# Weight places of a streamed mixture of experts: one w1 place for even and one for odd experts, one w2 place

## The reference

```
x = x + merged @ w_out
hf = rmsnorm(x, norm_ffn_g)
top_vals, top_idx = top_k(hf @ w_router + b_router, 4)     # of 32 experts
gates = softmax(top_vals)
# for each expert e, on the tokens that chose it (64 slots here):
gu  = xb @ w1[e] + b1[e]                # w1[e] is 1024 x 2048, 8 MB
act = (clip(up) + 1) * min(gate, 7) * sigmoid(1.702 * gate)
y  += gate_weight * (act @ w2[e] + b2[e])   # w2[e] is 1024 x 1024, 4 MB
out = rmsnorm(x + y, norm_final_g)
```

## Time and profile before

| | us |
|---|---|
| median of 3 runs | 1227.8 (1227.31 to 1229.17) |
| the profiled execution | 1227.92 |
| its span | 1225.9 |
| PE busy | 1169.0 (95% of the span) |
| DVE, ACT, POOL busy | 428.0, 207.7, 58.5 |
| moved by DMA | 461.79 MB, 377 GB/s over the span |

### The profile page before, as it was taken

How to read it: one execution, slowest core, us unless ns; L and a number is a source line. 1 busy time by engine, 2 the same in 40 slices (tenths; PEclk the granted TensorE clock), 3 DMA queues, 4 the chain that set the end, 5 groups by cost and what they waited for, 6 DMA issues and landing times.

```text
span 1225.9 us, 17199 instructions
## 1 busy us (share of the span) xinstructions
PE 1169.0 (95%) x7154; PEld 588.0 (48%) x7154; DVE 428.0 (35%) x741; ACT 207.7 (17%) x306; POOL 58.5 (5%) x43
## 2 busy tenths in 40 slices
PE   9999999999999999999999999999999899999897
PEld 8888888888643334333333333333333333333332
DVE  5886764655632223222222222222222222222222
ACT  6444553534400000000000000000000000000001
POOL 0850000000300000000000000000000000000000
PEclk9999999999999999999999999999999999999999
DMA  9756437877889999999999999999999999999996
GB/s 310 272 207 217 161 138 258 317 283 320 337 350 428 431 433 433 429 431 434 433 430 430 433 433 432 429 433 434 432 429 433 433 433 428 433 433 434 428 423 255
DMA packets 47522, 461.79 MB, mean 377 GB/s; under 512 B 4985, under 2 KB 6978, under 8 KB 32290
## 3 DMA queue, kind: packets, MB, share of 16 engines
q1 hardware_dynamic: 44760, 458.97, 89.9%
q10 hardware_dynamic: 2730, 2.36, 0.7%
HBM read 459.19 MB, written 1.07 MB: 375 GB/s over the span
## 4 chain that ended last, share of the span: by engine, by line
PE 66%; DMA 32%; DVE 1%; SPq 1%; ACT 0%; issue 0%; DVEq 0%; ACTq 0%
PE ps L1289 19%; DMA w_ring<-in_w 19%; PE ps L1355 12%; DMA A_QK<-in_w 6%; DMA xb_and_att<-in_w 6%; PE ps L1006 4%; PE ps L1444 4%; PE ps L1014 3%; PE ps L1012 3%; PE ps L1013 3%; PE ps L1263 2%; PE ps L1007 2%; PE ps L1026 1%; PE ps L1139 1%; PE ps L1141 1%; PE ps L1140 1%
## 5 line engine op out<-in xcount | busy, mean ns | idle before, releaser
L1289 PE MATMUL ps<-w_ring,A_W 128*64 128x512 f32 x1216 | 272.5, 596 | 28.9 <-DMA w_ring<-in_w 28.4
L1890 DVE TENSOR_SCALAR A_W<-ps 128x512 f32<-128x512 f32 x32 | 22.1, 692 | 478.2 <-PE ps L1289 478.2
L1289 PEld LDWEIGHTS ps<-w_ring,A_W 128*64 128x64 f32 x1216 | 84.8, 137 | 200.9 <-issue 160.2
L1355 PE MATMUL ps<-w_ring,A_W 128*64 128x512 f32 x608 | 137.9, 595 | 0.0
L1534 DVE TENSOR_TENSOR w_parts<-w_ring,w_parts 128x1024 fp32r<-128x1024 f32 x76 | 109.9, 1463 | 56.4 <-ACT w_parts L733 55.5
L1289 PE MATMUL ps<-A_QK,A_W 128*64 128x512 f32 x416 | 93.2, 595 | 9.3 <-DMA A_QK<-in_w 9.3
L918 ACT ACTIVATE A_W<-ps 128x512 f32<-128x512 f32 x31 | 18.5, 597 | 462.9 <-PE ps L1336 462.9
L1289 PE MATMUL ps<-xb_and_att,A_W 128*64 128x512 f32 x384 | 86.2, 596 | 9.4 <-DMA xb_and_att<-in_w 9.4
L733 ACT ACTIVATE w_parts<-w_ring 128x1024 fp32r<-128x1024 f32 x75 | 78.9, 1058 | 64.6 <-PE ps L1007 32.1
L914 ACT ACTIVATE A_W<-A_W 128x512 f32<-128x512 f32 x32 | 20.2, 631 | 359.8 <-DVE A_W L1890 359.8
L1006 PE MATMUL ps<-hT_both,w_parts 128*128 128x512 f32 x224 | 79.3, 399 | 0.0
(11 more groups left out here) (266 smaller groups left out, 1198.7 us busy)
## 6 DMA issues: line engine op xcount, KB each, us to landing
w_ring<-in_w SPq DMA_DIRECT2D x110, 2048.0 KB, 35.2
A_QK<-in_w SPq DMA_DIRECT2D x38, 2048.0 KB, 35.1
xb_and_att<-in_w SPq DMA_DIRECT2D x35, 2048.0 KB, 35.2
w_ring<-in_w_in SPq DMA_DIRECT2D x36, 1024.0 KB, 7.3
w_ring<-in_w SPq DMA_DIRECT2D x8, 1024.0 KB, 23.7
w_ring<-in_w_ret_branch SPq DMA_DIRECT2D x2, 2048.0 KB, 10.9
xb_and_att<-in_w SPq DMA_DIRECT2D x4, 1024.0 KB, 20.6
A_W<-in_w_out SPq DMA_DIRECT2D x1, 2560.0 KB, 13.0
```

The lines of the kernel that those rows point to most:

```text
L1289: mm = pe.matmul(o, XT[:, k, :], hidden_columns(tile[:, j, :], c), start=(k == 0), stop=(k == KC - 1))
L1355: mm = pe.matmul(ps[CAP * c:CAP * c + CAP, 3, :], lhs, w2_tile(flat)[:, q % W2_ROWS, c * HALF:(c + 1) * HALF], start=False, stop=(q == FQ ...
L1890: dve.tensor_scalar(gl, bank(0), LIMIT, None, ALU.min).then_inc(s.g, 1)
```

## The change

Three things are changed. First, the places: w1 of even experts has one place of four units (w1_flat), w1 of odd experts another (`w1_odd`, four units that lie next to each other from the end of `gr` to the end of A_QK), and w2 has one place of two units (w2_flat). A_W[:, 0:4096] (LATE_UNIT) now holds one unit of w2 of expert 1 and then one of expert 2. Second, the loops run over two experts instead of five, and PE's first four and SP's first six experts are written out. SP's list changes with it. In SP's loop w2 of expert e waits until both units of w2 of expert e-1 are used, and the two halves of w1 of expert e+2 stand behind it.

Third, the opening on PE, DVE, ACT and POOL: expert 0 is summed in PSUM banks 6 and 7 and reads its tokens from `XT_first`, `spread_gain` and the fill are gone (the gain is loaded by a transfer of 512 KB at the end of SP's list), the gather for expert 1 stands ahead of the fourth unit of expert 0, and ACT stores the second tile's residual after `activate` of expert 0 has read the banks.

```diff
-RING = 10
-TURN = 5
+W1_WORDS = W1_UNITS * UNIT_WORDS
+TURN = 2
...
+        w1_places = [w1_flat, w1_odd[:, :]]
+        LATE_UNIT = A_W[:, 0:UNIT_WORDS]
...
+        def w1_place(e, u):
+            return w1_places[e % 2][:, u * UNIT_WORDS:(u + 1) * UNIT_WORDS]
+        def w2_place(e, u):
+            if (e, u) in ((1, 0), (2, 1)):
+                return LATE_UNIT
+            if (e, u) == (1, 1):
+                return w2_part(0)
+            if (e, u) == (2, 0):
+                return w2_part(1)
+            return w1_part(u) if e == N_EXP - 1 else w2_part(u)
...
+        def load_w1_units(sp, e, units):
+            for u in units:
+                sp.wait_ge(s_used, w1_number(e - 2, u) + 1)
+                load_w1(sp, e, u)
+        def load_w1_pair(sp, e, k, u, used):
+            to = w1_places[k % 2][:, u * UNIT_WORDS:(u + 2) * UNIT_WORDS].rearrange("p (j n) -> p j n", j=PAIR_ROWS)
+            source = w1_both(e, u)
+            sp.wait_ge(s_used, used + w1_number(k - 2, u + 1) + 1)
+            for odd in range(2):
+                sp.dma_start(to[odd::2], source[odd::2]).then_inc(s_w1[k % 2][u // 2], 16)
+        def load_w2_pair(sp, e, k, used):
+            to, source = w2_flat.rearrange("p (j n) -> p j n", j=FQ), w2_both(e)
+            sp.wait_ge(s_used, used + w2_number(k - 1, 1) + 1)
+            for odd in range(2):
+                sp.dma_start(to[odd::2], source[odd::2]).then_inc(s_w2, 16)
...
             sp.wait_ge(s_wl, LAST_BRANCH + 4)
+            load_w2(sp, 1, 0)
+            sp.wait_ge(s_wu, LAST_BRANCH + UNITS)
             load_first(sp, 3)
-            sp.wait_ge(s_wu, LAST_BRANCH + UNITS)
-            load_w2(sp, 0, 1, 9)
             sp.wait_ge(s_wo, 3)
-            load_w2(sp, 0, 0, 8)
+            load_first(sp, 2)
             sp.wait_ge(s_x2, 2 * TT)
-            load_w1(sp, 2, 0, 10)
-            for u in range(HALF_UNITS):
...
+            load_w1(sp, 1, 0)
+            for u in range(W1_UNITS):
...
-            for i in range(1, TURN):
-                load_expert_w1(sp, i + 1, i + 1, 0)
-                load_expert_w2(sp, i, i, 0)
-            with sp.Fori(1, (N_EXP - 2) // TURN) as r:
-                for i in range(TURN):
-                    load_expert_w1(sp, r * TURN + i + 1, TURN + i + 1, (r - 1) * (TURN * E_UNITS))
-                    load_expert_w2(sp, r * TURN + i, TURN + i, (r - 1) * (TURN * E_UNITS))
...
+            load_w1_units(sp, 3, range(W1_UNITS))
+            sp.wait_ge(s_used, w2_number(0, 0) + 1)
+            load_w2(sp, 1, 1)
+            sp.wait_ge(s_used, w2_number(0, 1) + 1)
+            load_w2(sp, 2, 0)
+            load_w1_units(sp, 4, range(W1_UNITS))
+            sp.wait_ge(s_used, w2_number(1, 0) + 1)
+            load_w2(sp, 2, 1)
+            sp.wait_ge(s_used, w2_number(1, 1) + 1)
+            load_w2(sp, 3, 0)
+            load_w1_units(sp, 5, (0, 1))
+            sp.wait_ge(s_used, w2_number(2, 0) + 1)
+            load_w2(sp, 3, 1)
+            load_w1_units(sp, 5, (2, 3))
+            with sp.Fori(0, (N_EXP - 8) // TURN) as r:
+                for k in range(4, 4 + TURN):
+                    used = r * (TURN * E_UNITS)
+                    load_w2_pair(sp, r * TURN + k, k, used)
+                    load_w1_pair(sp, r * TURN + k + 2, k + 2, 0, used)
+                    load_w1_pair(sp, r * TURN + k + 2, k + 2, 2, used)
+            load_w1_pair(sp, N_EXP - 2, N_EXP - 2, 0, 0)
+            load_w2_pair(sp, N_EXP - 4, N_EXP - 4, 0)
+            load_w1_pair(sp, N_EXP - 2, N_EXP - 2, 2, 0)
+            load_w2_pair(sp, N_EXP - 3, N_EXP - 3, 0)
...
+            sp.wait_ge(s_lo, 2 * TT)
+            sp.dma_start(gain[:, :], bass.AP(g_final.tensor, 0, [[0, P], [1, D]])).then_inc(s_gain, 16)
...
                     if u == 2:
-                        hidden_bias(main, 0)
+                        hidden_bias(main, 0, FIRST_BANK)
                         second_scales()
-                        spread_gain()
...
+                        pe.wait_ge(s_lo, 2 * TT)
+                        gather(main, 1, scaled=True)
...
             hidden_first()
-            pe.wait_ge(s_lo, 2 * TT)
-            gather(main, 1, scaled=True)
-            pe.wait_ge(main.scales, 2)
-            fill(3, 8)
-            pe.wait_ge(s_res, 2 * TT)
```

More of the change, by code:

```diff
@@ L392, in w2_part @@
             return w2_flat[:, n * UNIT_WORDS:(n + 1) * UNIT_WORDS]
[L394 to L397, removed]
+        w1_places = [w1_flat, w1_odd[:, :]]
+        LATE_UNIT = A_W[:, 0:UNIT_WORDS]
+        LAST_W2 = ((N_EXP - 2, 0), (N_EXP - 2, 1), (N_EXP - 1, 0))
         def hidden_columns(row, c):
@@ L428, in w2_number @@
             return W1_UNITS + E_UNITS * e + W1_UNITS + u if e < N_EXP - 1 else N_UNITS - W2_UNITS + u
[L430 to L438, removed]
@@ L440, in load_w2 @@
-        def load_w2(sp, e, u, n):
-            flat, landed, _ = place(n)
-            sp.dma_start(w2_tile(flat), w2_source(e, u)).then_inc(landed, 16)
-        def load_first(sp, u):
[L445 to L473, removed]
+        def w1_place(e, u):
+            return w1_places[e % 2][:, u * UNIT_WORDS:(u + 1) * UNIT_WORDS]
@@ L609, in _ @@
-            for n, (e, u) in enumerate(((N_EXP - 2, 0), (N_EXP - 2, 1), (N_EXP - 1, 0))):
-                sp.wait_ge(s_used, w2_number(e, u) - RING + 1)
-                flat = place(w2_number(e, u))[0]
+                sp.dma_start(to[:, 1, :], source[:, 1, :]).then_inc(landed, 16)
+            load_w1_units(sp, 3, range(W1_UNITS))
[3 more added lines that the diff above has]
+            load_w2(sp, 2, 0)
@@ L902, in _, with store_residual @@
                                accum_out=gden[:, t:t + 1]).then_inc(s_tke, 1)
-            for t in range(TT):
-                if t:
-                    act.wait_ge(s_gainp, 1)
-                    act.wait_ge(s_lo, 2 * TT)
-                    act.activation(gain[:, :], bank(6, 2), ACT.Copy).then_inc(s_gain, 1)
-                    act.wait_ge(s_gain, 1)
+            def store_residual(t):
                 for h in range(2):
@@ L920, in _ @@
             act.activation(warm, warm, ACT.Sigmoid)
+            act.wait_ge(s_res, 2)
             sigmoid(main, 0)
+            act.wait_ge(main.chain, 1)
+            store_residual(1)
+            act.wait_ge(s_res, 2 * TT)
             store_act(main, 0)
@@ L1363, in down_unit, with project_down @@
                 return mm
-            def project_down(i, first, rounds=0):
+            def project_down(i, k, more):
                 down_bias(main, i)
                 for u in range(W2_UNITS):
-                    flat, landed, count = place(first + u)
-                    pe.wait_ge(landed, 2 * rounds + count)
-                    down_unit(flat, u).then_inc(s_used, 1)
+                    landed, count = w2_landed(k, u)
+                    pe.wait_ge(landed, more + count)
+                    down_unit(w2_place(k, u), u).then_inc(s_used, 1)
                     if u == 0:
@@ L1379, in hidden_last @@
                     pe.wait_ge(s_unit[u], 32)
-                    hidden_unit(place(w1_number(N_EXP - 1, u))[0], u).then_inc(s_used, 1)
+                    hidden_unit(w1_place(N_EXP - 1, u), u).then_inc(s_used, 1)
                     if u == 0:
@@ L1465, in second_scales @@
                 gather_scales().then_inc(main.gathered, 1)
-            def spread_gain():
-                pe.wait_ge(s_grows, 32)
-                for c in range(KC):
-                    mm = pe.matmul(psf[:, 6 * HALF + c * P:6 * HALF + (c + 1) * P],
-                                   ident[0:KC, c:c + 1].broadcast_to([KC, P]), g_rows[:, :], start=(c % 4 == 0),
-                                   stop=True, skip_group_check=True)
-                mm.then_inc(s_gainp, 1)
             fill(0, 6)
@@ L1887, in down_done, with activate @@
                 dve.wait_ge(s_used, i * E_UNITS + W1_UNITS + E_UNITS)
-            def activate(s, i, stored=None, scaled=False):
-                dve.tensor_scalar(gl, bank(0), LIMIT, None, ALU.min).then_inc(s.g, 1)
-                dve.tensor_scalar(ul, bank(1), LIMIT, -LIMIT, ALU.min, ALU.max).then_inc(s.chain, 1)
-                if stored is not None and not scaled:
+            def activate(s, i, stored=None, b=0):
+                dve.tensor_scalar(gl, bank(b), LIMIT, None, ALU.min).then_inc(s.g, 1)
+                dve.tensor_scalar(ul, bank(b + 1), LIMIT, -LIMIT, ALU.min, ALU.max).then_inc(s.chain, 1)
+                if stored is not None:
                     dve.wait_ge(s.x, stored)
```

128 lines of the change are left out of this document (73 added, 55 removed).

## The result

The changed kernel takes 1246.0 us (median of 4, 1245.83 to 1246.46) against 1228.47 us before, a ratio of 1.0143 (95% interval 1.0127 to 1.0159). The forecast was 1245.6, in a range of 1238 to 1253. The profiled execution took 1245.83 us with a span of 1243.7, 17.8 us more than before. In the changed kernel L1313 is what L1289 was (a unit of w1), L1380 what L1355 was (w2).

What follows compares the result with a forecast made beforehand. Transfers were taken to bound the kernel. The profiled 1227.92 us plus 15.7 for a later last pair (stream +9.8, order at the end +5.9) and 2 for the clock gave 1245.6 us, range 1238 to 1253.

Steps and rivals of the forecast that it cites:

- The bound: Whole kernel: DMA transfers set the time, full at about 432 GB/s, one 2 MB unit taking 4.856 us.
- PE's opening: Start of PE's work: expert 1 starts at 336.33 instead of 339.45, 3.12 us earlier; by itself nothing at the end.
- One more unit ahead: Stream at 339.3 to 343.9: fifteen units under way instead of fourteen, so the stop there goes, -4.6 us.
- SP's list: SP's loop: the next issue waits for the end of w2 of expert 3, so DMA idles 15.5 us, 426.7 to 442.2.
- The allowance of 3.6 us: Added to the stream's sum for ramp and landing, between 1.1 and 4.7; last w1 unit of expert 30 lands at 1174.2.
- The order at the end: Behind SP's loop: w1 of expert 30 goes ahead of w2 of expert 28, so PE reaches its last pair +5.9 us later.
- The clock: PE after the 8.5 us wait: w2 of expert 28 starts at 1.2 GHz, +2 us, between 0 and 7.5.
- The order at the end costs nothing: Rival at the end: PE makes up or the queue lets the later transfer through; +9.8 alone, 1237.7 us, chance 0.12.
- The clock stays down longer: Rival at the end: w2 of 28 and first half of 30 at half speed, up to 1259 us; 0.13 shared with loop gaps.
- the opening isn't earlier: Rival at PE's start: expert 1 starts at 339.45 as before, all behind 3.1 later, 1248.7 us, chance 0.04.
- More gaps in several experts: Rival in the loop: the 3 us margin fails, leaving small gaps for several experts; 1251 to 1259, 0.13 shared with slow clock.
- The hole is covered: Rival at 442.2: the stream runs on from 339.3 without a stop; 1223.3 us with the end made up for, chance 0.05.

Runs made afterwards that it cites:

- The finest schedule: Changed kernel with w2 of expert 28 issued before w1 of 30, and 4, 3, 2, 2, 1, 1 w1 units ahead of w2 for experts 4 to 9: 1223.54 us.
- the run with PE kept busy: Changed kernel with PE's last two loop experts written out and 130 filling matmuls ahead of w2 of expert 28: 1243.72 us.
- the stop filled: Changed kernel with both w1 pairs of e+2 ahead of w2 of e for experts 4 and 5, the first pair for 6 to 9: 1235.65 us.
- the stop at 339 put back: Changed kernel with the last unit of expert 2 held back until two units of expert 1 are used: 1245.86 us.
- PE held back: Changed kernel with 56 filling matmuls (about 3.1 us) on PE between expert 0 and expert 1: 1249.99 us.
- both mended: Changed kernel with w1 pairs ahead of w2 (both for experts 4, 5; first for 6 to 9) and w2 of 28 before w1 of 30: 1226.39 us.
- half of w1 ahead everywhere: Changed kernel with SP's loop issuing the first w1 pair of e+2 ahead of w2 of e, in all experts from 4 on: 1235.51 us.

## Why the prediction was right, point by point

- *The bound.* Transfers, at 4.856 us a unit. After: 433 and 432 GB/s in the long stretches, PE waits 64.2 us in all (66 forecast).
- *PE's opening.* 3.12 us earlier forecast, expert 1 at 336.33; it starts at 335.87, since PE was already 0.4 us earlier where the changed lines begin (330.89 against 331.33).
- *One more unit ahead.* No stop at 339 to 344, as forecast, and swallowed by the later stop, as the run that put it back shows. Alone it was to be a gain of 4.6 us; no run has it alone. The finest schedule, which has the other changes too, is 5.1 us ahead of the kernel before.
- *SP's list.* Idle from 426.7 to 442.2 forecast, from 427.3 to 442.0 seen. The slowing at 411 to 414 (382 GB/s, 0.3 us) was counted as nothing. Closing the stop by 9.5 us gave 10.5 back; closing it by 15.0 and opening 6.0 elsewhere gave 10.4.
- *The allowance of 3.6 us* between sum and landing was chosen between 1.1 and 4.7, nearer to 4.7 without a row that says how near. w2 of expert 28 was to land at 1164.5 and did at 1164.2; with the start at 442.0 that makes the term 3.5 (1164.2 + 9.7 - 442.0 - 728.4). What it consists of no run shows, so a hit this close is luck within a range of 3.6 us.
- *The order at the end.* +5.9 forecast, 5.7 measured (8.0 less 2.3). The wait was to last 8.5 us and lasted 8.4.
- *The clock.* +2 chosen between 0 and 7.5; the row shows 5.72 - 3.53 = 2.2, the run with PE kept busy 2.3. That the clock would fall followed from the row; its price did not, and +2 was luck too: with the same wait of 8.4 us the unit takes 5.2, 5.7, 5.8 and 6.5 us in four runs (the stop filled, the changed kernel, the stop at 339 put back, PE held back), a price of 1.7 to 3.0 us. The Trainium skill ("TensorE: Matmul & The Clock Gate", on HAM oscillation) says that matmuls behind a long wait for a DMA start cold; the trace agrees, with a granted clock of 0.50 from 1164 to 1168.
- *The rivals.* "The order at the end costs nothing" falls with 8.0 us. "The clock stays down longer" falls with one slow unit, "the opening isn't earlier" with the 335.87. "More gaps in several experts" falls: there is only one more, at 1171 to 1175, since w2 of expert 29 waits until the slowed w2 of 28 is used (issued at 1173.97). My sum had overlooked it: it let the ten units behind the last pair follow in 48.6 us without a stop, though by its own numbers w2 of 28 is used up only at 1172.0 (1164.5 + 7.5) and the stream is dry from 1170.6. The stop is 4 x (1 - 25/432) = 3.8 us. It costs nothing here, because PE is behind the stream there, but the slack at the end shrank: the stream ends at about 1226.5 instead of the 1222.8 of my sum. "The hole is covered" became real only in the mended list, 1223.5 against the 1223.3 that I had given for it.

## What to carry to other kernels

When transfers set the time, draw the queue's supply as a line: how many units may be asked for against how many are through, for the phase in which the compute engine lags and for the one in which it waits. A list that is right in the second (all of an expert's loads behind one wait) can run dry in the first, and where it does, no compute engine waits: the loss shows there only as a lower rate, and as waits tens of microseconds later. A wait in a single in-order list holds back every load behind it whose place is already free; put in front of it as many as the lead allows, and step that number down as the lead shrinks.

## What was not expected of the hardware

The granted clock can fall in much shorter waits than the 8.4 us one. In the run with half of w1 ahead everywhere PE waited 2.66 us ahead of w2 of expert 28 and the next unit took 4.9 us instead of 3.5; one of 1.22 us at the same line didn't do it (3.6 us), nor did those of 1.43 us in the changed kernel. The length of the wait alone doesn't decide it: eleven waits of 2.66 to 2.68 us in that run were followed by a slow unit and one of 2.57 us was not; with the stop filled one of 2.31 us was, and in the run with both mended one of 2.67 us was not. The stretches of the first run around the wait:

```profile
1150.00:1154.00 4.00, 1.85 (x10) 0.50 (x6) 2.82 (x6) 0.00 (x0) 0.00 (x0) 0.98 1.09 467
1154.00:1158.00 4.00, 3.49 (x10) 1.10 (x12) 0.00 (x0) 0.00 (x0) 0.00 (x0) 0.59 0.95 410
1158.00:1162.00 4.00, 4.00 (x21) 1.26 (x19) 0.42 (x1) 0.00 (x0) 0.00 (x0) 1.00 0.91 393
```

As long as the stream is full such a fall is hidden by the next wait: in that run the times leave nothing for the ten falls before the last. Behind the last wait it counts in full. And where SP's next issue hangs on the slowed w2, it lengthens a stop: with the stop filled PE ended w2 of expert 5 at 498.1, with both mended at 495.1, and the stream stopped for 3.6 and 1.6 us; of the 3.0 us between them 1.6 are the slow unit and 1.4 a later landing (489.03 against 487.65).

Nor had I expected that a kernel's spread can come from a marginal stop: 1223.59 to 1229.54 us with two stops of about 1.5 us in the fastest run, 1222.32 to 1223.96 without. The record gives a likely reason: in the ten executions the mean granted clock is by and large the lower the longer the time, from 0.999 in the fastest over 0.997 and 0.998 at 1225.6 to 1226.0 and 0.996 at 1226.8 to 1227.4 down to 0.995 in the slowest, and stands at 0.999 in all five without the stops. A clock that falls in some executions behind the waits at w2 and not in others, with the longer stop behind it, would do this. It isn't shown, since only the fastest of the ten left a trace.
